# Stick-breaking attention: the running product over pairs of neighbouring keys, with GpSimd folding the odd key's factor into the even beta

## The chip, the cores and the metric

One NeuronCore of a Trainium2 chip runs the whole kernel in one launch. The metric is device time in microseconds (us), the median over runs of the same compiled kernel; lower is better.

## What is computed

A decoder block with two branches over 2048 positions and 1024 channels, all in float32. The branch that matters here is stick-breaking attention, with 8 heads of 128 channels. For each query t and each earlier key s,

```
logits    = einsum('bthd,bshd->bhts', q_blk, k) * head_dim ** -0.5
beta      = sigmoid(logits)
A[t, s]   = beta[t, s] * prod_{s < j < t} (1 - beta[t, j])
y_b       = A @ v
```

Keys at or after the query have weight 0. Before it come an RMSNorm, one input projection of 9 times 1024 columns and the other branch (gMLP); after it, the two output projections, a gated merge, a residual add and a final RMSNorm.

## The kernel before, in words

The kernel has four stages, one after the other: `norm_and_project` (the input projection, results stored to HBM as transposed arrays such as `k_T` and `vb_T`), `gate_and_project_a`, `attention`, and `merge_and_project_out`. TensorE multiplies float32 as three products of rounded parts (hi by hi, hi by lo, lo by hi), so most tiles exist as a pair hi and lo.

**Projection.** In `norm_and_project`, TensorE fills eight PSUM banks in turn; ScalarE takes each finished bank through a function into `o_sb` (L375 for the outputs that are stored alone, Copy for q, k and v) and issues its store.

**Attention.** For each head, the queries are cut into 16 rows of 128 (i = 0 to 15). Row i has (i + 1) * 128 keys, cut into pieces of up to 512 keys from the right (`z_pieces`). That makes 40 pieces per head, 320 in all: 28 of 512 keys and 4 each of 384, 256 and 128 keys per head. Each piece goes through five steps on four engines:

1. TensorE: the logits into one of three PSUM banks `z_ps` (L1287 to L1289), and on the diagonal block the mask (L1291).
2. ScalarE: sigmoid of the logits into `slot[i]` (L1177), which holds the betas; then sigmoid of the negated logits, which is 1 - beta, into `rest[i % 4]` (L1184). Each of the four `rest` buffers holds a whole row and ends in a column of ones. Before it writes the first piece of a row ScalarE waits until GpSimd has finished the row four earlier (`weighted`).
3. VectorE: `scan` (L1232), a running product from right to left in place over `rest`, which starts from the element to the right of the piece.
4. GpSimd: `weights` (L1143), beta times the product of everything to its right, in place in `slot[i]`.
5. TensorE: later, when all pieces of a row are done, it transposes 128x128 blocks of the row (L1320) into `t_ps`. ScalarE rounds them to `wT_hi` (L1207), VectorE takes the remainder `wT_lo` (L1244), and TensorE multiplies by v (L1331 to L1333). VectorE's gate product for a finished group of 512 queries is L1262.

VectorE also takes the lo part of the next head's q and k (L1221, eight pieces of 512 per head, both inputs in SBUF) and of v (L1240).

The order is written out by hand. `head_order` interleaves logits, splits and products of one head into one list, and every engine walks that same list: Z is a piece's logits and sigmoids, W its scan and weights, V and B the transposes, P the products, QK the splits, Y the gate product. Before the first head, 24 pieces (rows 0 to 11) run alone (`early`); within a head the last four rows run first and then the first twelve rows of the next head; the eighth head has only its own last 16 pieces. Each engine runs its instructions in order, so an instruction that waits holds up everything behind it. `P` is 128, `CW` and `ZW` are 512, `S` is 2048.

Of the kernel before, what the change touches and what calls it, by code (L numbers as in the profile page):

```python
# [17 lines left out]
ACT = mybir.ActivationFunctionType  # L18
# [128 lines left out]
def make_identity(pool, ident, zeroed, done):  # L147
# [4 lines left out]
                       pattern=[[-1, P]], channel_multiplier=1).then_inc(done, 1)  # L152

def norm_and_project(nc, x, norm_in, w_in, w_o_gmlp, s, carried):
# [13 lines left out]
    with ExitStack() as memory:  # L170
# [108 lines left out]
        def _(act):  # L279
# [83 lines left out]
            for n, (_, func, dst) in enumerate(single):  # L363
                before = UZ - 1 + n * PER

                def one_output(t):
                    for b in range(2):
                        for i in range(BANKS):
                            m, c = divmod(i, NC)
                            row = ((2 * t + b) * 2 + m) * P  # L370
                            step = 2 * (t + before) + b
                            act.wait_ge(pj.full[b][i], t + (before + 1))

                            wait_past(act, stored[i], 16 * (step - (0 if i < NC else 2 * (UZ - 1))))
                            act.activation(o_sb[:, i], banks[i][:, :], func).then_inc(pj.free[i], 1)  # L375
                            act.wait_ge(pj.free[i], step + 2)
                            act.dma_start(dst[bass.ds(row, P), c * CW:(c + 1) * CW], o_sb[:, i])\
                                .then_inc(stored[i], 16)

                if n == 0:  # L380
                    turns_from_first(act, PER, one_output)
                else:
                    with act.Fori(0, PER) as t:
                        one_output(t)
# [589 lines left out]
def attention(nc, w_o_sb, s, carried):  # L974
# [6 lines left out]
    W_BUFS = 4  # L981
    RESTS = 4
    assert PRODUCTS % W_BUFS == 0

    with ExitStack() as memory:
# [11 lines left out]

        rest = [sc.sb(f"rest{n}", [P, S + 1]) for n in range(RESTS)]

# [12 lines left out]
        z_full = sc.sem("z_full")  # L1012
        z_read = sc.sem("z_read")
        scanned = sc.sem("scanned")
        weighted = sc.sem("weighted")
# [114 lines left out]
        def _(pool):  # L1130
# [3 lines left out]

            pool.affine_select(out=mask[:, :], in_=mask[:, :], compare_op=ALU.is_gt, fill=MASKED, base=0,
                               pattern=[[-1, P]], channel_multiplier=1).then_inc(mask_done, 1)

            def weights(i, at, width, h, n):

                left = S - (i + 1) * P + at  # L1140
                a, r = slot[i][:, at:at + width], rest[i % RESTS]
                pool.wait_ge(scanned, PIECES * h + (n + 1))
                pool.tensor_tensor(a, a, r[:, left + 1:left + width + 1], ALU.mult).then_inc(weighted, 1)  # L1143

# [12 lines left out]
        def _(act):  # L1157
# [10 lines left out]
            def sigmoids(i, at, width, h, n):  # L1168

                src = z_ps[n % Z_BANKS][:, 0:width]  # L1170
                w = (i + 1) * P
                right = S - w + at
                act.wait_ge(z_full, PIECES * h + (n + 1))
                if at + width == w:
                    if not first_head(h):
                        act.wait_ge(turned, STEPS * h + (steps_until(i // QT) - STEPS))
                act.activation(slot[i][:, at:at + width], src, ACT.Sigmoid, scale=SCALE)  # L1177
                if at + width == w:

                    if i >= RESTS:  # L1180
                        act.wait_ge(weighted, PIECES * h + pieces_before(i - RESTS + 1))
                    elif not first_head(h):
                        act.wait_ge(weighted, PIECES * h + (pieces_before(NT + i - RESTS + 1) - PIECES))
                act.activation(rest[i % RESTS][:, right:right + width], src, ACT.Sigmoid, scale=-SCALE)\  # L1184
                    .then_inc(z_read, 1)

# [22 lines left out]
            for part in range(len(SPLITS)):  # L1209
                split_qk(0, part)  # L1210
            act.wait_ge(ones_set, RESTS)
            for n, e in enumerate(early):
# [4 lines left out]
        def _(dve):  # L1217
# [6 lines left out]
            def scan(i, at, width, h, n):  # L1224

                dve.wait_ge(z_read, PIECES * h + (n + 1))
                left = S - (i + 1) * P + at
                r = rest[i % RESTS]
                if at + width < (i + 1) * P:
                    dve.wait_ge(scanned, PIECES * h + n)  # L1230
                backwards = r[:, left:left + width][:, ::-1]
                dve.tensor_tensor_scan(out=backwards, data0=backwards, data1=backwards,  # L1232
                                       initial=r[:, left + width:left + width + 1], op0=ALU.mult,
                                       op1=ALU.bypass).then_inc(scanned, 1)
# [30 lines left out]
            for n in range(RESTS):  # L1265
                dve.memset(rest[n][:, S:S + 1], 1.0).then_inc(ones_set, 1)
            dve.wait_ge(ident_done, 1)
            dve.tensor_copy(ident_r[:, :], ident[:, :]).then_inc(consts, 1)
            dve.wait_ge(mask_done, 1)
            dve.tensor_copy(mask_r[:, :], mask[:, :]).then_inc(consts, 1)  # L1270
            for part in range(len(SPLITS)):
                split_qk(0, part)
# [375 lines left out]
```

## Time and profile before

| | |
|---|---|
| runs | 3024.46 us median of 3 (3023.23 to 3026.32) |
| profiled execution, first to last instruction | 3029.8 us |
| its own time around the span | not listed apart from the span |
| TensorE busy | 2814.0 us (93%) |
| VectorE busy | 1141.3 us (38%) |
| ScalarE busy | 881.2 us (29%) |
| GpSimd busy | 457.6 us (15%) |
| mean granted TensorE clock | 0.965 of full |

Busy time counts an instruction from its recorded start to its recorded end, time in which it is held up included. Two instructions that follow each other on VectorE or GpSimd without a wait can overlap by some hundredths of a microsecond in the records. "Idle before" is how long the engine stood empty before an instruction, with the instruction that released it behind the arrow. The shares above are over the whole span; attention fills only some 740 us of it.

### The profile page before, as it was taken

How to read it: one execution, taken by the hardware profiler on the slowest of the kernel's cores; microseconds unless marked ns; L12 is line 12 of the kernel's file. 1: busy time of each engine (PE TensorE's matmuls, PEld its weight loads, DVE VectorE, ACT ScalarE, POOL GpSimd, SP SyncE). 2: the span in 40 equal slices, each digit the busy share in tenths (PEclk: the TensorE clock that was granted, in tenths of full speed). 3: DMA queues.
4: the chain of work that ended last, by engine and by line, in shares of the span. 5: the costliest groups of instructions: out<-in, count | busy, mean ns of one | idle time of the engine just before them, and what ended most of it. 6: DMA issues, size and time to landing. Idle time of an engine off the chain costs nothing. (4 is left out here: it accounts for less than half of the span.)

```text
span 3029.8 us, 38475 instructions
## 1 busy us (share of the span) xinstructions
PE 2814.0 (93%) x14664; PEld 2392.2 (79%) x14664; DVE 1141.3 (38%) x1315; ACT 881.2 (29%) x1655; POOL 457.6 (15%) x432
## 2 busy tenths in 40 slices
PE   7999999999999999999996999688888888799998
PEld 5888888888888888888885999566666766689997
DVE  4310110000000000000003443999999999743333
ACT  5411111111111111111112221666766766521111
POOL 1111100000000000000001221644444444200000
PEclk9999999999999999999997999898989989999999
DMA  4310122122112212221115443111212110253332
GB/s 135 94 55 28 55 94 74 65 74 75 68 71 76 76 62 76 76 76 62 62 48 160 133 144 121 56 63 46 69 38 69 62 62 17 96 193 111 125 111 69
DMA packets 192585, 246.14 MB, mean 81 GB/s; under 512 B 9872, under 2 KB 141968, under 8 KB 189456
## 3 DMA queue, kind: packets, MB, share of 16 engines
q1 hardware_dynamic: 145040, 161.50, 16.7%
q10 hardware_dynamic: 47488, 83.90, 7.4%
q8 instruction: 32, 0.52, 0.1%
q14 instruction: 25, 0.20, 0.0%
HBM read 153.10 MB, written 92.27 MB: 81 GB/s over the span
## 5 line engine op out<-in xcount | busy, mean ns | idle before, releaser
L127 PE MATMUL in_bank<-in_h_hi,in_w_hi 128*128 128x512 f32 (+1 forms) x2304 | 897.7, 390 | 0.0
L129 PE MATMUL in_bank<-in_h_hi,in_w_lo 128*128 128x512 f32 (+1 forms) x2304 | 896.6, 389 | 0.0
L128 PE MATMUL in_bank<-in_h_lo,in_w_hi 128*128 128x512 f32 (+1 forms) x2304 | 896.5, 389 | 0.0
L118 DVE CAST in_w_hi<-in_w_stage 128x2048 fp32r<-128x2048 f32 x36 | 44.2, 1226 | 1292.6 <-PE in_bank L129 1292.6
L129 PEld LDWEIGHTS in_bank<-in_h_hi,in_w_lo 128*128 128x128 f32 x2304 | 432.6, 188 | 89.8
L127 PEld LDWEIGHTS in_bank<-in_h_hi,in_w_hi 128*128 128x128 f32 x2304 | 432.8, 188 | 89.5
L128 PEld LDWEIGHTS in_bank<-in_h_lo,in_w_hi 128*128 128x128 f32 x2304 | 432.6, 188 | 89.6
L1232 DVE TENSOR_TENSOR_SCAN att_rest<-att_rest 128x512 f32<-128x512 f32 (+3 forms) x320 | 445.5, 1398 | 36.1 <-ACT att_rest L1184 33.5
L375 ACT ACTIVATE in_o_sb<-in_bank 128x512 f32<-128x512 f32 x224 | 134.0, 598 | 1055.7 <-PE in_bank L129 1055.7
L1143 POOL TENSOR_TENSOR att_slot<-att_slot,att_rest 128x512 f32<-128x512 f32 (+3 forms) x320 | 343.0, 1077 | 378.7 <-DVE att_rest L1232 378.7
L1320 PE MATMUL att_t_ps<-att_ident,att_slot 128*128 128x128 f32 x1088 | 185.3, 288 | 61.6 <-DVE att_wT_lo L1244 51.6
L1177 ACT ACTIVATE att_slot<-att_z_ps 128x512 f32<-128x512 f32 (+3 forms) x320 | 173.1, 541 | 189.4 <-PE att_z_ps L1291 128.9
L1320 PEld LDWEIGHTS att_t_ps<-att_ident,att_slot 128*128 128x128 f32 x1088 | 128.1, 145 | 117.2 <-DVE att_wT_lo L1244 85.9
L1244 DVE TENSOR_TENSOR att_wT_lo<-att_t_ps,att_wT_hi 128x512 fp32r<-128x512 f32 (+1 forms) x320 | 185.7, 586 | 7.3 <-ACT att_wT_hi L1207 7.2
L610 POOL MEMSET a_minus_half<- 128x1 f32 x1 | 0.1, 98 | 1220.6 <-POOLq L47 1220.6
L1207 ACT ACTIVATE att_wT_hi<-att_t_ps 128x512 fp32r<-128x512 f32 (+1 forms) x320 | 172.5, 543 | 38.4 <-PE att_t_ps L1320 37.0
L1184 ACT ACTIVATE att_rest<-att_z_ps 128x512 f32<-128x512 f32 (+3 forms) x320 | 172.2, 539 | 2.4 <-POOL att_slot L1143 2.3
L1287 PE MATMUL att_z_ps<-att_k_hi,att_q_hi 128*128 128x512 f32 (+3 forms) x320 | 128.6, 402 | 45.0 <-DVE att_k_lo L1221 44.1
L1331 PE MATMUL att_y_ps<-att_wT_hi,att_v_hi 128*128 128x512 f32 (+1 forms) x320 | 147.6, 461 | 17.5 <-DVE att_wT_lo L1244 17.5
L1563 PE MATMUL b_p_ps<-b_y_hi,b_wo_hi 128*128 128x256 f32 x512 | 145.8, 285 | 14.5 <-DVE b_y_lo L1504 14.5
L838 PE MATMUL a_p_ps<-a_ya_hi,a_wo_hi 128*128 128x256 f32 x512 | 147.3, 288 | 4.0 <-DVE a_ya_lo L724 4.0
L839 PE MATMUL a_p_ps<-a_ya_lo,a_wo_hi 128*128 128x256 f32 x512 | 145.7, 285 | 0.0
(116 smaller groups left out, 3698.4 us busy)
## 6 DMA issues: line engine op xcount, KB each, us to landing
in_w_stage<-in_w_in SPq DMA_DIRECT2D x72, 512.0 KB, 4.4
carried_buffer<-in_x SPq DMA_DIRECT2D x32, 512.0 KB, 3.5
uz_T<-in_o_sb ACTq DMA_DIRECT2D x32, 256.0 KB, 2.7
va_T<-in_o_sb ACTq DMA_DIRECT2D x32, 256.0 KB, 2.4
q_T<-in_o_sb ACTq DMA_DIRECT2D x32, 256.0 KB, 2.4
k_T<-in_o_sb ACTq DMA_DIRECT2D x32, 256.0 KB, 2.4
vb_T<-in_o_sb ACTq DMA_DIRECT2D x32, 256.0 KB, 2.4
zb_T<-in_o_sb ACTq DMA_DIRECT2D x32, 256.0 KB, 2.4
```

Of the source, the lines that this page charges most:

```text
L127: pe.matmul(bank[:, :], hi, self.act_hi[:, k, cols], start=(k == 0), stop=False)
L128: pe.matmul(bank[:, :], hi, self.act_lo[:, k, cols], start=False, stop=False)
L129: mm = pe.matmul(bank[:, :], lo, self.act_hi[:, k, cols], start=False, stop=(k == KT - 1))
L838: pe.matmul(out, wo_hi[:, j, ks], ya_hi[:, b, j], start=(j == 0), stop=False)
L1143: pool.tensor_tensor(a, a, r[:, left + 1:left + width + 1], ALU.mult).then_inc(weighted, 1)
L1177: act.activation(slot[i][:, at:at + width], src, ACT.Sigmoid, scale=SCALE)
L1184: act.activation(rest[i % RESTS][:, right:right + width], src, ACT.Sigmoid, scale=-SCALE)\
L1207: act.activation(wT_hi[k % W_BUFS][:, c0:], t_bank(t)[:, c0:], ACT.Copy).then_inc(hi_copied, 1)
L1232: dve.tensor_tensor_scan(out=backwards, data0=backwards, data1=backwards, initial=r[:, left + width:left + width + 1], op0=ALU.mult, op1=A ...
L1244: dve.tensor_tensor(wT_lo[n][:, c0:], t_bank(t)[:, c0:], wT_hi[n][:, c0:].bitcast(F32), ALU.subtract).then_inc(lo_copied, 1)
L1320: ins = pe.transpose(out, slot[i][:, kt * P:(kt + 1) * P], ident[:, :])
L1331: pe.matmul(bank[:, c0:], v_hi[:, ks], hi[:, c0:], start=(kt == 0), stop=False)
```

## The change

The keys are stored apart by parity: inside each block of 128 keys the 64 even ones come first, then the 64 odd ones. ScalarE writes `k_T` and `vb_T` in that order when it empties the PSUM banks, and the mask is built in that order. `rest` becomes six buffers of one piece each instead of four of one row each. VectorE first multiplies the even and the odd half of a piece of `rest` into `pairs` (half as many columns, four buffers of a row each, ending in a column of ones), waits for that on its own semaphore, and then scans `pairs`. The wait for GpSimd's work on the row four earlier moves from ScalarE to VectorE; ScalarE now waits until the piece six earlier has been read by VectorE (`paired`) and GpSimd (`folded`). GpSimd first multiplies the even betas by the odd neighbour's 1 - beta (the fold, which needs only ScalarE's output), and after the scan multiplies all betas of the piece by the product of the pairs to their right, each of which is read twice through a stride of 0.

```diff
+def by_parity(keys):
+    return keys.rearrange("p (b m t) -> p b t m", t=2, m=P // 2)
...
+def by_parity_to(keys):
+    return keys.rearrange("p (b t m) -> p b t m", t=2, m=P // 2)
...
 def norm_and_project(nc, x, norm_in, w_in, w_o_gmlp, s, carried):
...
-                            act.activation(o_sb[:, i], banks[i][:, :], func).then_inc(pj.free[i], 1)
+                            if dst in (s["k_T"], s["vb_T"]):
+                                act.activation(by_parity_to(o_sb[:, i]), by_parity(banks[i][:, :]), func)\
+                                    .then_inc(pj.free[i], 1)
+                            else:
+                                act.activation(o_sb[:, i], banks[i][:, :], func).then_inc(pj.free[i], 1)
...
-        rest = [sc.sb(f"rest{n}", [P, S + 1]) for n in range(RESTS)]
+        rest = [sc.sb(f"rest{n}", [P, ZW]) for n in range(R_BUFS)]
+        pairs = [sc.sb(f"pairs{n}", [P, S // 2 + 1]) for n in range(RESTS)]
...
             def weights(i, at, width, h, n):
-                left = S - (i + 1) * P + at
-                a, r = slot[i][:, at:at + width], rest[i % RESTS]
+                left = (S - (i + 1) * P + at) // 2
+                nb, half = width // P, width // 2
+                a = slot[i][:, at:at + width].rearrange("p (b t m) -> p b t m", t=2, m=P // 2)
+                r = rest[n % R_BUFS][:, 0:width].rearrange("p (b t m) -> p b t m", t=2, m=P // 2)
+                pool.wait_ge(z_read, PIECES * h + (n + 1))
+                pool.tensor_tensor(a[:, :, 0], a[:, :, 0], r[:, :, 1], ALU.mult).then_inc(folded, 1)
                 pool.wait_ge(scanned, PIECES * h + (n + 1))
-                pool.tensor_tensor(a, a, r[:, left + 1:left + width + 1], ALU.mult).then_inc(weighted, 1)
+                pool.wait_ge(folded, PIECES * h + (n + 1))
+                after = pairs[i % RESTS][:, left + 1:left + half + 1].rearrange("p (b m) -> p b m", m=P // 2)
+                pool.tensor_tensor(a, a, after.unsqueeze(2).to_broadcast([P, nb, 2, P // 2]), ALU.mult)\
+                    .then_inc(weighted, 1)
...
                 act.activation(slot[i][:, at:at + width], src, ACT.Sigmoid, scale=SCALE)
-                if at + width == w:
-                    if i >= RESTS:
-                        act.wait_ge(weighted, PIECES * h + pieces_before(i - RESTS + 1))
-                    elif not first_head(h):
-                        act.wait_ge(weighted, PIECES * h + (pieces_before(NT + i - RESTS + 1) - PIECES))
-                act.activation(rest[i % RESTS][:, right:right + width], src, ACT.Sigmoid, scale=-SCALE)\
-                    .then_inc(z_read, 1)
+                before = last_user(n, PIECES, R_BUFS)
+                if before >= 0 or not first_head(h):
+                    act.wait_ge(folded, PIECES * h + (before + 1))
+                    act.wait_ge(paired, PIECES * h + (before + 1))
+                act.activation(rest[n % R_BUFS][:, 0:width], src, ACT.Sigmoid, scale=-SCALE).then_inc(z_read, 1)
...
             def scan(i, at, width, h, n):
                 dve.wait_ge(z_read, PIECES * h + (n + 1))
-                left = S - (i + 1) * P + at
-                r = rest[i % RESTS]
+                left, half = (S - (i + 1) * P + at) // 2, width // 2
+                q = pairs[i % RESTS]
+                r = rest[n % R_BUFS][:, 0:width].rearrange("p (b t m) -> p b t m", t=2, m=P // 2)
+                if at + width == (i + 1) * P:
+                    if i >= RESTS:
+                        dve.wait_ge(weighted, PIECES * h + pieces_before(i - RESTS + 1))
+                    elif not first_head(h):
+                        dve.wait_ge(weighted, PIECES * h + (pieces_before(NT + i - RESTS + 1) - PIECES))
+                dve.tensor_tensor(q[:, left:left + half].rearrange("p (b m) -> p b m", m=P // 2),
+                                  r[:, :, 0], r[:, :, 1], ALU.mult).then_inc(paired, 1)
+                dve.wait_ge(paired, PIECES * h + (n + 1))
                 if at + width < (i + 1) * P:
                     dve.wait_ge(scanned, PIECES * h + n)
-                backwards = r[:, left:left + width][:, ::-1]
+                backwards = q[:, left:left + half][:, ::-1]
                 dve.tensor_tensor_scan(out=backwards, data0=backwards, data1=backwards,
-                                       initial=r[:, left + width:left + width + 1], op0=ALU.mult,
+                                       initial=q[:, left + half:left + half + 1], op0=ALU.mult,
                                        op1=ALU.bypass).then_inc(scanned, 1)
```

## Rows read from the trace of the kernel before

**Rows 1.** Busy time by engine: the first pieces of attention, then its body.

```profile
core 0: us, PE busy (x) PEld busy (x) DVE busy (x) ACT busy (x) POOL busy (x), PEclk, DMA share, GB/s
...
1895.00:1940.00 45.00, 23.79 (x104) 17.62 (x104) 42.05 (x37) 26.88 (x62) 37.21 (x26) 0.77 0.13 53
1940.00:2640.00 700.00, 586.08 (x3161) 476.29 (x3161) 651.70 (x734) 465.67 (x993) 306.17 (x297) 0.92 0.17 57
```

**Rows 2.** Who waited for whom, 1940 to 2640 us: total us, times, longest.

```profile
POOL att_slot L1143 <- DVE att_rest L1232: 371.1, 272, 4.4
...
PEld att_t_ps L1320 <- DVE att_wT_lo L1244: 85.9, 98, 1.7
...
DVE att_rest L1232 <- ACT att_rest L1184: 32.2, 36, 1.3
```

**Rows 3.** VectorE in order of time in the body: start us, duration us, what.

```profile
2204.35 0.66 DVE L1244 TENSOR_TENSOR att_wT_lo<-att_t_ps,att_wT_hi 128x512 fp32r<-128x512 f32 x1
2204.93 1.75 DVE L1232 TENSOR_TENSOR_SCAN att_rest<-att_rest 128x512 f32<-128x512 f32 x1
2206.60 0.66 DVE L1244 TENSOR_TENSOR att_wT_lo<-att_t_ps,att_wT_hi 128x512 fp32r<-128x512 f32 x1
```

**Rows 4.** GpSimd in the same stretch.

```profile
2204.51 1.09 POOL L1143 TENSOR_TENSOR att_slot<-att_slot,att_rest 128x512 f32<-128x512 f32 x1 [1.16 <-DVE att_rest L1232]
```

**Rows 5.** VectorE instructions in order of time with no GpSimd work beside them.

```profile
1896.89 0.69 DVE L1221 TENSOR_TENSOR att_q_lo<-carried_buffer,att_q_hi 128x512 fp32r<-128x512 f32 x1
...
1941.02 1.27 DVE L1232 TENSOR_TENSOR_SCAN att_rest<-att_rest 128x512 f32<-128x512 f32 x1
...
1949.55 0.74 DVE L1232 TENSOR_TENSOR_SCAN att_rest<-att_rest 128x256 f32<-128x256 f32 x1
...
1984.80 1.02 DVE L1232 TENSOR_TENSOR_SCAN att_rest<-att_rest 128x384 f32<-128x384 f32 x1 [0.16 <-ACT att_rest L1184]
...
2212.55 0.48 DVE L1232 TENSOR_TENSOR_SCAN att_rest<-att_rest 128x128 f32<-128x128 f32 x1 [0.61 <-ACT att_rest L1184]
```

**Rows 6.** Order of time at a second place: VectorE, then GpSimd.

```profile
1999.93 2.01 DVE L1232 TENSOR_TENSOR_SCAN att_rest<-att_rest 128x512 f32<-128x512 f32 x1
...
1999.77 1.09 POOL L1143 TENSOR_TENSOR att_slot<-att_slot,att_rest 128x512 f32<-128x512 f32 x1 [1.50 <-DVE att_rest L1232]
```

**Rows 7.** Order of time among the first pieces: VectorE, then GpSimd.

```profile
1915.56 1.86 DVE L1232 TENSOR_TENSOR_SCAN att_rest<-att_rest 128x512 f32<-128x512 f32 x1
...
1914.33 2.01 POOL L1143 TENSOR_TENSOR att_slot<-att_slot,att_rest 128x512 f32<-128x512 f32 x1
...
1916.30 2.01 POOL L1143 TENSOR_TENSOR att_slot<-att_slot,att_rest 128x512 f32<-128x512 f32 x1
```

**Rows 8.** VectorE in the last stage; L1519 waits for L1517 on its own engine.

```profile
2803.27 0.42 DVE L1517 TENSOR_TENSOR b_gate<-b_p_ps,b_gate 128x256 f32<-128x256 f32 x1 [0.35 <-PE b_p_ps L1565]
2803.73 0.42 DVE L1519 TENSOR_TENSOR b_gate<-b_gate,carried_buffer 128x256 f32<-128x256 f32 x1
```

**Rows 9.** GpSimd in order of time: pieces of 256 and of 128 keys.

```profile
1993.62 0.64 POOL L1143 TENSOR_TENSOR att_slot<-att_slot,att_rest 128x256 f32<-128x256 f32 x1 [0.62 <-DVE att_rest L1232]
...
2213.12 0.41 POOL L1143 TENSOR_TENSOR att_slot<-att_slot,att_rest 128x128 f32<-128x128 f32 x1 [0.78 <-DVE att_rest L1232]
```

**Rows 10.** VectorE groups by form, all of attention: busy us, mean ns, idle.

```profile
L1232 DVE TENSOR_TENSOR_SCAN att_rest<-att_rest 128x512 f32<-128x512 f32 x224 | 358.8, 1603 | 8.1 <-ACT att_rest L1184 5.6
...
L1221 DVE TENSOR_TENSOR att_q_lo<-carried_buffer,att_q_hi 128x512 fp32r<-128x512 f32 x32 | 33.7, 1058 | 0.0
```

**Rows 11.** GpSimd L626, both operands as blocks of 128: ns min/median/max.

```profile
L626 POOL TENSOR_TENSOR a_y<-a_y,a_bias x16: 2357/2400/4323, 1638.6 to 1855.6; 128x1024 f32<-128x1024 f32 x16
```

**Rows 12.** GpSimd group by form in the projection stage, VectorE mostly idle.

```profile
L275 POOL TENSOR_TENSOR in_o_sb<-in_o_sb 128x512 f32<-128x512 f32 x24 | 33.7, 1405 | 227.5 <-ACT in_o_sb L356 227.5
```

**Rows 13.** ScalarE L375, 1000 to 1100 us, and its idle time, in us and times.

```profile
L375 ACT ACTIVATE in_o_sb<-in_bank x19: 598/598/601, 1000.8 to 1098.7; 128x512 f32<-128x512 f32 x19
...
  PE in_bank L129: 90.7, 19
```

More of the change, by code:

```diff
@@ L152, in make_identity, with in_parity @@
                        pattern=[[-1, P]], channel_multiplier=1).then_inc(done, 1)
+def by_parity(keys):
+    return keys.rearrange("p (b m t) -> p b t m", t=2, m=P // 2)
+def in_parity(keys):
+    return keys.rearrange("p (t m) -> p t m", t=2)
+def by_parity_to(keys):
+    return keys.rearrange("p (b t m) -> p b t m", t=2, m=P // 2)
 def norm_and_project(nc, x, norm_in, w_in, w_o_gmlp, s, carried):
@@ L982, in attention @@
     RESTS = 4
+    R_BUFS = 6
     assert PRODUCTS % W_BUFS == 0
@@ L1013, in attention @@
         z_read = sc.sem("z_read")
+        paired = sc.sem("paired")
+        folded = sc.sem("folded")
         scanned = sc.sem("scanned")
@@ L1133, in _ @@
             pool.wait_ge(mask_zeroed, 1)
-            pool.affine_select(out=mask[:, :], in_=mask[:, :], compare_op=ALU.is_gt, fill=MASKED, base=0,
-                               pattern=[[-1, P]], channel_multiplier=1).then_inc(mask_done, 1)
+            pool.affine_select(out=in_parity(mask[:, :]), in_=in_parity(mask[:, :]), compare_op=ALU.is_gt,
+                               fill=MASKED, base=0, pattern=[[-1, 2], [-2, P // 2]],
+                               channel_multiplier=1).then_inc(mask_done, 1)
             def weights(i, at, width, h, n):
-                left = S - (i + 1) * P + at
-                a, r = slot[i][:, at:at + width], rest[i % RESTS]
+                left = (S - (i + 1) * P + at) // 2
[4 more added lines that the diff above has]
+                pool.tensor_tensor(a[:, :, 0], a[:, :, 0], r[:, :, 1], ALU.mult).then_inc(folded, 1)
                 pool.wait_ge(scanned, PIECES * h + (n + 1))
-                pool.tensor_tensor(a, a, r[:, left + 1:left + width + 1], ALU.mult).then_inc(weighted, 1)
+                pool.wait_ge(folded, PIECES * h + (n + 1))
+                after = pairs[i % RESTS][:, left + 1:left + half + 1].rearrange("p (b m) -> p b m", m=P // 2)
+                pool.tensor_tensor(a, a, after.unsqueeze(2).to_broadcast([P, nb, 2, P // 2]), ALU.mult)\
+                    .then_inc(weighted, 1)
             def body(h, last):
@@ L1171, in sigmoids @@
                 w = (i + 1) * P
-                right = S - w + at
                 act.wait_ge(z_full, PIECES * h + (n + 1))
@@ L1210, in _ @@
                 split_qk(0, part)
-            act.wait_ge(ones_set, RESTS)
             for n, e in enumerate(early):
@@ L1265, in _ @@
             for n in range(RESTS):
-                dve.memset(rest[n][:, S:S + 1], 1.0).then_inc(ones_set, 1)
+                dve.memset(pairs[n][:, S // 2:S // 2 + 1], 1.0).then_inc(ones_set, 1)
             dve.wait_ge(ident_done, 1)
@@ L1270, in _ @@
             dve.tensor_copy(mask_r[:, :], mask[:, :]).then_inc(consts, 1)
+            dve.wait_ge(ones_set, RESTS)
             for part in range(len(SPLITS)):
```

## Prediction

> **What bounds the kernel now.** The change touches attention, so I read the busy time of that stage first. In its body, 1940 to 2640 us, VectorE is busy 651.7 of 700 us, TensorE 586.1, ScalarE 465.7, GpSimd 306.2 [rows 1]. The list of waits agrees: TensorE's weight loads for the transposes stand empty behind `wT_lo`, VectorE's last step before a product, for 85.9 us, while VectorE itself waits for its input for only 32.2 us. GpSimd waits 371.1 us for scans, so it has room [rows 2]. VectorE sets the pace, and what is spared or added in its queue moves the end. By busy time alone GpSimd looks like a free helper.
>
> The second question is what VectorE's busy time is made of. In order of time, a steady piece of 512 keys goes: `wT_lo` at 2204.35, scan at 2204.93 for 1.75 us, the next `wT_lo` at 2206.60, a period of 2.25 us [rows 3]. The same scan with no GpSimd work beside it takes 1.27 us [rows 5]. The other 0.48 us is a stall. GpSimd's multiply starts at 2204.51 [rows 4]; a scan that ends at 2206.68 and needs 1.27 us began its work at 2205.41, which is 0.90 us after the multiply's start. A second place says the same: multiply at 1999.77, scan issued at 1999.93 and 2.01 us long [rows 6], so it worked from 2000.67, again 0.90 us after the multiply's start. So the scan, which reads two operands from SBUF, and GpSimd's multiply exclude each other for most of the multiply. It goes the other way too: in the first pieces, scan behind scan, the multiply is recorded at 2.01 us and the scan at 1.86, and multiplies start 1.97 us apart [rows 7], which is 1.07 + 0.90. I take 1.07 us as the scan's share (1.27 less its fixed part, about 0.20) and 0.90 as the multiply's. `wT_lo` reads one operand from PSUM and stays at 0.66 us beside a multiply [rows 3, 4]. What this kernel has too little of is therefore not only VectorE's time but the turns that the two engines take, and the change adds GpSimd work there.
>
> **The change on VectorE.** The scan of 512 columns becomes one of 256: 0.74 us instead of 1.27 [rows 5]. Added is a multiply of 256 columns from SBUF. L1519, also two SBUF operands, takes 0.42 us at that width, and starts 0.04 us after the end of the instruction it waits for on its own engine [rows 8]. Alone, then: 0.42 + 0.04 + 0.74 = 1.20 against 1.27 us, a gain of 0.07 us per piece. Halving the scan brings almost nothing, since the pairing costs what the shorter scan spares.
>
> **The stalls.** Take the end of a scan as 0. The multiply of that piece starts at 0.08 (2204.51 against 2204.43 [rows 3, 4]) and excludes VectorE until 0.98. VectorE does `wT_lo`, then issues the pairing at 0.50, which stalls to 0.98 as the scan did before, works to about 1.25 and is recorded to 1.40. The scan could start at 1.44. But GpSimd is done with the multiply at 1.17 and has the next fold ready in its queue, since the fold needs only ScalarE's output. The fold has 256 columns. A GpSimd multiply goes from 0.41 us at 128 columns to 0.64 at 256 [rows 9] and 1.09 at 512 [rows 4], 1.77 ns a column, so 256 columns exclude for 0.45 us. It gets its turn when the pairing lets go, at 1.25, and holds to 1.70. The scan runs from 1.70 to 2.44. The period was 2.25, so the piece costs 0.19 us more: -0.07 for the shorter work and +0.26 for the fold's turn. The average piece stalls less than that one (mean scan 1603 ns, so 0.33 us [rows 10]), but that is the multiply's stall, which stays; the fold's comes on top. The other account agrees: where both engines are saturated, turns per piece go from 1.07 + 0.90 = 1.97 to 0.27 + 0.53 + 0.45 + 0.90 = 2.15 us, +0.18, and the 24 first pieces get that.
>
> **The sum.** 224 pieces of 512 at +0.19 are 43 us. Narrower ones go by the same lines (pairing 0.15 us + 1.05 ns a column, from 0.42 at 256 [rows 8] and 0.69 at 512 [rows 5]; scan 0.22 us + 2.06 ns; fold 1.77 ns, of which 0.19 us passes before the scan is ready). For 384 keys: 0.35 + 0.04 + 0.61 + 0.15 = 1.15 against 1.02. For 256: 0.28 + 0.04 + 0.48 + 0.04 = 0.84 against 0.74. For 128: 0.22 + 0.04 + 0.35 = 0.61 against 0.48. Together +0.36 for 32 of each, 12 us. The 56 splits that run beside GpSimd also read twice from SBUF: 1.06 us on average [rows 10] against 0.69 alone [rows 5], a stall of 0.37. GpSimd's turns rise from 0.90 of 2.25 us to 1.35 of 2.44, 1.38 times the share, so +0.14 each, 8 us. The sum is +63 us. On the profiled execution, span 3029.8 us, that is 3093; the median of the runs shown is 5.3 us shorter, so 3087.
>
> **What costs nothing.** ScalarE empties the projection's banks with a strided read for k and v: 64 instructions of 598 ns, and between 19 of them in 100 us it waited 90.7 us for TensorE [rows 13]. Even twice as long they stay under TensorE; without that cover, 64 times 0.6 is 38 us. No stores or loads are added or moved, so SP's queue is as before. ScalarE's removed wait on `weighted` was not felt, and its new waits reach back four to six pieces, some 9 us or more, behind work that GpSimd and VectorE do in order; behind them would stand the sigmoids and `wT_hi` copies. VectorE's new wait on `weighted` reaches back at least three pieces. If GpSimd lagged so far, `wT_lo` would be late behind it, and TensorE after it. TensorE's own instructions do not change.
>
> **What the trace does not show.** GpSimd has no instruction here that steps over blocks of 64 or reads through a stride of 0. Downwards, contiguous rows give 1.77 ns a column, and nothing suggests less. Upwards, L626 with blocks of 128 takes 2.40 us for 1024 columns at the median [rows 11], 2.2 ns a column beyond the 0.41 us of 128. A contiguous multiply of 512 in the projection takes 1.41 us [rows 12], longer than here by 0.32 with no VectorE work beside it, so GpSimd's fixed part isn't certain either. I take 1.77, since it is this very line in this stage. The scan of 256 and the pairing are bounded from below by the rows at that width.
>
> A rule bears on the turns. The Trainium skill, SBUF — State Buffer, section "Who interferes with whom", says that GpSimd and a VectorE instruction with two SBUF inputs contend, and that whoever starts first keeps the shared ports for its whole instruction. The trace agrees on who contends, and differs on how long: the scan worked 0.19 us before the multiply's recorded end. What the rule would give by whole records is the third rival.
>
> **Rivals.**
> - *The fold finds a free turn (faster), 0.13.* The price that decides is the 0.26 us; below 0.07 the change gains. The place is the gap under `wT_lo`, 0.58 us, where VectorE does not need a turn, but the multiply fills it, being released by the scan just ended. Where something else (a gate product, a v split) stands between, the fold can fit too. Were it always so: -0.07 for 224, and -0.02, +0.06 and +0.13 for 32 each, -10 us: 3014. A lesser share of free turns gives no change, 0.07.
> - *GpSimd is slower on blocks, 0.20.* At 2.2 ns a column the multiply excludes for 1.14 us and the fold for 0.57: pairing +0.24, scan +0.12, in all +0.55 per piece of 512, 123 us, half of the addition (0.18) on 96 narrower ones with the 12, 29 us, and the splits 10: 3187. Rows 11 speak for it, the flat L1143 against. The Trainium skill, GPSIMD Engine Reference, section 3.1, puts a two-input elementwise operation at about 2.6 cycles an element, which at its 1.2 GHz I estimate as 2.2 ns; L1143's 1.77 disagrees, L626 does not.
> - *Turns last for whole records, 0.03.* Pairing from 1.17 to 1.59, fold to 2.23, scan to 2.97: +0.72 us for 224, 161 us, with the rest about 3215. Against it: before, such a scan would have ended at 2206.87 and ended at 2206.68.
> - *The change doesn't shorten the scan.* If a scan cost the same at half the width it would add 0.5 us a piece; the widths in [rows 5] rule that out.
>
> **How the numbers follow.** The forecast, 3087, has a chance of 0.57. The faster case holds 0.13, no change 0.07, GpSimd slower on blocks 0.20 and whole records 0.03. Faster or slower by 0.2% (6 us) is about what a measurement of this kernel can tell. So faster 0.13, same 0.07, slower 0.80. The range takes in the no-gain case and reaches halfway and more into the slower GpSimd: 3012 to 3160.
>
> **What would show each step.** Scans of 256 near 0.74 us alone, with a mean of some 1.0; pairings of 0.42 alone, with a mean near 0.75; folds at 0.64 alone and longer beside VectorE; GpSimd busy over 600 us; the period of a steady piece 2.4 us and the idle time of transposes behind `wT_lo` longer. ScalarE in the projection may take longer and TensorE there must not wait. Wrong is the forecast if the pairing's or the scan's records show no stall, if folds exceed 0.7 us with VectorE idle, or if the body of attention is not some 60 us longer.

## The result, and the profile after

The changed kernel takes 3120.32 us (median of 4 runs, 3118.78 to 3122.11) against 3025.39 us for the kernel before in the same comparison. The ratio is 1.0311, with a 95% interval of 1.0295 to 1.0326: slower by 95 us. The forecast was 3087, slower by 63.

The page of the changed kernel: busy time, share of the span and instructions of each engine.

```profile
span 3120.4 us, 39891 instructions
...
PE 2836.5 (91%) x14664; PEld 2397.0 (77%) x14664; DVE 1233.5 (40%) x1635; ACT 885.6 (28%) x1655; POOL 683.2 (22%) x752
```

The profiled run took 3122.11 us around a span of 3120.4. VectorE's busy time rose by 92.2 us from 1141.3, GpSimd's by 225.6 from 457.6. By stretches (busy us of each engine, clock, DMA), which answer to [rows 1]:

```profile
core 0: us, PE busy (x) PEld busy (x) DVE busy (x) ACT busy (x) POOL busy (x), PEclk, DMA share, GB/s
...
1895.00:1940.00 45.00, 29.98 (x103) 21.51 (x103) 41.42 (x56) 28.46 (x63) 35.05 (x44) 0.68 0.15 56
1940.00:2640.00 700.00, 525.57 (x2755) 416.27 (x2756) 664.86 (x927) 418.66 (x895) 483.86 (x547) 0.92 0.15 49
```

In the same 700 us of attention, VectorE is a little fuller than before (664.9 us against 651.7) and TensorE is less busy (525.6 us against 586.1). Who waited for whom, 1940 to 2720 us (total, times, longest):

```profile
POOL att_slot L1175 <- DVE att_pairs L1269: 185.2, 272, 1.6
PEld att_t_ps L1358 <- DVE att_wT_lo L1281: 150.7, 149, 2.8
...
DVE att_pairs L1263 <- ACT att_rest L1214: 23.9, 29, 1.3
```

GpSimd's spare time behind scans shrank, and TensorE waits longer for `wT_lo`: 150.7 us over 780 us, against 85.9 over 700 in [rows 2]. A steady piece, VectorE in order of time (start, duration), which answers to [rows 3]:

```profile
2283.41 0.66 DVE L1281 TENSOR_TENSOR att_wT_lo<-att_t_ps,att_wT_hi 128x512 fp32r<-128x512 f32 x1
2283.99 0.95 DVE L1263 TENSOR_TENSOR att_pairs<-att_rest 128x256 f32<-128x256 f32 x1
2284.98 1.11 DVE L1269 TENSOR_TENSOR_SCAN att_pairs<-att_pairs 128x256 f32<-128x256 f32 x1
2286.01 0.66 DVE L1281 TENSOR_TENSOR att_wT_lo<-att_t_ps,att_wT_hi 128x512 fp32r<-128x512 f32 x1
```

and GpSimd, which answers to [rows 4]:

```profile
2283.57 1.10 POOL L1175 TENSOR_TENSOR att_slot<-att_slot,att_pairs 128x512 f32<-128x512 f32 x1 [0.62 <-DVE att_pairs L1269]
2284.62 0.92 POOL L1171 TENSOR_TENSOR att_slot<-att_slot,att_rest 128x256 f32<-128x256 f32 x1
2286.17 1.10 POOL L1175 TENSOR_TENSOR att_slot<-att_slot,att_pairs 128x512 f32<-128x512 f32 x1 [0.63 <-DVE att_pairs L1269]
```

The period from `wT_lo` to `wT_lo` is 2.60 us, where it was 2.25. The pairing is recorded at 0.95 us and needs 0.42; the scan at 1.11 and needs 0.75. The fold, issued 1.05 us after the multiply, is recorded at 0.92 us and needs 0.72 or 0.73 (both shown further below). Each of the three stands still for a while behind an instruction of the other engine. VectorE's groups in attention (count, busy us and mean ns, idle before) show the same on average; these answer to [rows 10], and the groups of 192 and 128 columns are left out:

```profile
L1269 DVE TENSOR_TENSOR_SCAN att_pairs<-att_pairs 128x256 f32<-128x256 f32 x224 | 237.1, 1058 | 7.9
L1263 DVE TENSOR_TENSOR att_pairs<-att_rest 128x256 f32<-128x256 f32 x224 | 184.5, 824 | 3.6 <-ACT att_rest L1214 3.5
...
L1249 DVE TENSOR_TENSOR att_q_lo<-carried_buffer,att_q_hi 128x512 fp32r<-128x512 f32 x32 | 33.8, 1061 | 0.0
...
L1249 DVE TENSOR_TENSOR att_k_lo<-carried_buffer,att_k_hi 128x512 fp32r<-128x512 f32 x32 | 26.7, 839 | 0.0
...
L1269 DVE TENSOR_TENSOR_SCAN att_pairs<-att_pairs 128x64 f32<-128x64 f32 x32 | 19.6, 613 | 1.1
...
L1263 DVE TENSOR_TENSOR att_pairs<-att_rest 128x64 f32<-128x64 f32 x32 | 13.9, 434 | 12.1 <-ACT att_rest L1214 11.9
```

VectorE's last gate product of attention moved from 2639.90 to

```profile
2730.30 0.69 DVE L1299 TENSOR_TENSOR att_y<-att_y_ps,att_zb 128x512 f32<-128x512 f32 x1 [1.47 <-PE att_y_ps L1371]
```

so by 90.4 us. The spans of the two profiled runs differ by 90.6 us, so the whole loss lies inside attention. ScalarE's strided copies in the projection are the same 598 ns as the plain ones (ns min/median/max, first and last start):

```profile
L391 ACT ACTIVATE in_o_sb<-in_bank x64: 598/598/601, 746.7 to 1089.3; 128x512 f32<-128x512 f32 x64
```

### The profile page after: what moved, and what is told of

Same layout as the page of the kernel before. It is cut to its first block and busy times, and to the rows that moved or that the text cites. A ratio compares the mean times of both kernels' runs of the same rounds, so it can differ in the third digit from the quotient of the medians.

```text
span 3120.4 us, 39891 instructions
## 1 busy us (share of the span) xinstructions
PE 2836.5 (91%) x14664; PEld 2397.0 (77%) x14664; DVE 1233.5 (40%) x1635; ACT 885.6 (28%) x1655; POOL 683.2 (22%) x752
## 5 line engine op out<-in xcount | busy, mean ns | idle before, releaser
L1175 POOL TENSOR_TENSOR att_slot<-att_slot,att_pairs 128x512 f32<-128x512 f32 (+3 forms) x320 | 317.5, 992 | 193.1 <-DVE att_pairs L1269 186.6
L1269 DVE TENSOR_TENSOR_SCAN att_pairs<-att_pairs 128x256 f32<-128x256 f32 (+3 forms) x320 | 305.0, 953 | 11.3
L394 ACT ACTIVATE in_o_sb<-in_bank 128x512 f32<-128x512 f32 x160 | 95.7, 598 | 745.9 <-PE in_bank L129 745.8
L1171 POOL TENSOR_TENSOR att_slot<-att_slot,att_rest 128x256 f32<-128x256 f32 (+3 forms) x320 | 263.4, 823 | 48.6 <-ACT att_rest L1214 48.5
L1358 PEld LDWEIGHTS att_t_ps<-att_ident,att_slot 128*128 128x128 f32 x1088 | 129.2, 147 | 185.2 <-DVE att_wT_lo L1281 150.7
L1263 DVE TENSOR_TENSOR att_pairs<-att_rest 128x256 f32<-128x256 f32 (+3 forms) x320 | 244.5, 764 | 24.7 <-ACT att_rest L1214 24.4
L1214 ACT ACTIVATE att_rest<-att_z_ps 128x512 f32<-128x512 f32 (+3 forms) x320 | 171.0, 535 | 12.1 <-POOL att_slot L1171 12.1
```

Of the source, the lines that this page charges most:

```text
L1171: pool.tensor_tensor(a[:, :, 0], a[:, :, 0], r[:, :, 1], ALU.mult).then_inc(folded, 1)
L1175: pool.tensor_tensor(a, a, after.unsqueeze(2).to_broadcast([P, nb, 2, P // 2]), ALU.mult)\
L1263: dve.tensor_tensor(q[:, left:left + half].rearrange("p (b m) -> p b m", m=P // 2), r[:, :, 0], r[:, :, 1], ALU.mult).then_inc(paired, 1)
L1358: ins = pe.transpose(out, slot[i][:, kt * P:(kt + 1) * P], ident[:, :])
```

## The experiments

Two theories were to be told apart. **Turns**: VectorE instructions with two SBUF operands and GpSimd instructions that read SBUF exclude each other, and the fold adds to that. The rivals: **the pairing** (an added instruction with a wait and strided operands costs by itself), and **GpSimd's time** (its queue holds the pace, whatever it does). Each kernel below was timed beside the kernel before on the same chip; the ratios are against that one. The kernel before took 3019.55 to 3025.39 us (medians) in these comparisons, so a difference between two kernels of different comparisons carries a few us of uncertainty.

**Without the fold.**

```diff
-                pool.wait_ge(z_read, PIECES * h + (n + 1))
-                pool.tensor_tensor(a[:, :, 0], a[:, :, 0], r[:, :, 1], ALU.mult).then_inc(folded, 1)
...
-                pool.wait_ge(folded, PIECES * h + (n + 1))
...
-                    act.wait_ge(folded, PIECES * h + (before + 1))
```

> The changed kernel with GpSimd's fold left out (the even betas lack their neighbour's factor), everything else kept. Theory (turns): the fold's turn at the shared reads is what stalls the scan; without it the scan of 256 is back at about 0.75 us, the pairing stays near 0.95 us, the steady period falls from 2.60 to about 2.25 us and the time to 3015 to 3040 us. Rival (the pairing itself, its wait and the strided operands cost): the time stays above 3090 us.

Measured: 3019.34 us, ratio 0.999 (0.9981 to 1.0). The pairing, its wait, the half scan, the strided copies and the new buffers cost nothing and gain nothing in sum. VectorE in order of time:

```profile
2202.06 0.67 DVE L1277 TENSOR_TENSOR att_wT_lo<-att_t_ps,att_wT_hi 128x512 fp32r<-128x512 f32 x1
2202.64 0.96 DVE L1259 TENSOR_TENSOR att_pairs<-att_rest 128x256 f32<-128x256 f32 x1
2203.63 0.75 DVE L1265 TENSOR_TENSOR_SCAN att_pairs<-att_pairs 128x256 f32<-128x256 f32 x1
2204.30 0.67 DVE L1277 TENSOR_TENSOR att_wT_lo<-att_t_ps,att_wT_hi 128x512 fp32r<-128x512 f32 x1
```

and GpSimd in the same stretch:

```profile
2202.22 1.09 POOL L1172 TENSOR_TENSOR att_slot<-att_slot,att_pairs 128x512 f32<-128x512 f32 x1 [1.15 <-DVE att_pairs L1265]
```

The scan is 0.75 us, unstalled, the pairing still 0.96 behind the multiply, the period 2.24 to 2.25. Without the fold the whole loss is gone. The groups show that the sum of nothing is made of a gain and a loss:

```profile
L1265 DVE TENSOR_TENSOR_SCAN att_pairs<-att_pairs 128x256 f32<-128x256 f32 x224 | 184.3, 823 | 7.9
L1259 DVE TENSOR_TENSOR att_pairs<-att_rest 128x256 f32<-128x256 f32 x224 | 153.9, 687 | 5.8 <-ACT att_rest L1210 4.9
```

With the gap of 40 ns a piece of 512 keys takes 1550 ns of VectorE where the scan took 1603, a gain of 12 us over 224 pieces. The 96 narrower pieces lose 22 us by the same sum over their groups (the narrowest takes 400 + 40 + 606 ns where its scan took 657). The splits are 6 us shorter, and the pairings wait 27.1 us for ScalarE where the scans waited 33.5.

**A GpSimd instruction of the same length that reads nothing**, in the fold's place.

```diff
-                pool.wait_ge(z_read, PIECES * h + (n + 1))
-                pool.tensor_tensor(a[:, :, 0], a[:, :, 0], r[:, :, 1], ALU.mult).then_inc(folded, 1)
+                pool.memset(filler[:, 0:width * 5 // 4], 0.0).then_inc(folded, 1)
```

> The changed kernel with the fold replaced by a GpSimd memset of a scratch tile, 1.25 times the piece's width, about 0.6 us for a full piece: GpSimd is occupied as long as by the fold, but reads nothing from SBUF (the fold's product is left out). Theory (turns are for reads): as without the fold, 3015 to 3050 us. Rival (GpSimd's time or its queue holds the pace, whatever it does): 3100 us and more, as the changed kernel.

Measured: 3021.85 us, ratio 0.9999 (0.9989 to 1.0008). GpSimd in order of time:

```profile
2203.74 1.09 POOL L1175 TENSOR_TENSOR att_slot<-att_slot,att_pairs 128x512 f32<-128x512 f32 x1 [0.57 <-DVE att_pairs L1269]
2204.77 0.63 POOL L1171 MEMSET att_filler<- 128x640 f32 x1
```

and VectorE:

```profile
2204.16 0.96 DVE L1263 TENSOR_TENSOR att_pairs<-att_rest 128x256 f32<-128x256 f32 x1
2205.15 0.75 DVE L1269 TENSOR_TENSOR_SCAN att_pairs<-att_pairs 128x256 f32<-128x256 f32 x1
```

The memset holds GpSimd for 0.63 us, nearly as long as an unstalled fold, just where the fold was, under the end of the pairing and the start of the scan, and the scan is 0.75 us. On average too, scans of 256 take 823 ns with the memset and 823 without it. GpSimd's time is not what costs here; its reading is. The Trainium skill, SBUF — State Buffer, section "Who interferes with whom", says that a VectorE instruction with two SBUF inputs contends with a GpSimd instruction that reads SBUF and not with one that only writes. This run agrees with it.

**The kernel before with one more GpSimd multiply**, of half the piece's width into a scratch tile.

```diff
+                pool.wait_ge(z_read, PIECES * h + (n + 1))
+                pool.tensor_tensor(filler[:, 0:width // 2], slot[i][:, at:at + width // 2], ident[:, 0:1].to_broadcast([P, width // 2]),
+                                   ALU.mult).then_inc(folded, 1)
                 pool.wait_ge(scanned, PIECES * h + (n + 1))
+                pool.wait_ge(folded, PIECES * h + (n + 1))
```

> The kernel before with one more GpSimd multiply of half a piece's width per piece, from slot into a scratch tile, placed and waited for as the fold is; VectorE's work untouched, output unchanged. Theory (turns): the extra multiply costs the kernel before about as much as the whole change did: each steady scan stalls some 0.3 us more, 3090 to 3130 us. Rival (the pairing costs, GpSimd has room: it idled 371 us): within 10 us of the kernel before, 3025 us.

Measured: 3093.49 us, ratio 1.0231 (1.0211 to 1.025). The size is as the theory had it, without any pairing, but the loss takes another form than I expected. The mean scan of 512 fell to 1473 ns; instead GpSimd was stalled, its groups (count, busy us, mean ns)

```profile
L1149 POOL TENSOR_TENSOR att_slot<-att_slot,att_rest 128x512 f32<-128x512 f32 x224 | 337.7, 1508 | 32.1
L1145 POOL TENSOR_TENSOR att_filler<-att_slot,att_ident 128x256 f32<-128x256 f32 x224 | 247.8, 1106 | 0.0
```

being 0.4 and nearly 0.5 us longer than alone, so that GpSimd fell behind (it is busy 584.0 of the 620 us from 1940 to 2560) and the wait before `rest` is overwritten was felt (waits, 1940 to 2600 us):

```profile
DVE att_rest L1238 <- ACT att_rest L1190: 100.0, 38, 5.4
ACT att_rest L1190 <- POOL att_slot L1149: 93.6, 25, 6.3
```

A scan of 512 keeps its turn for some 1.07 us (as worked out in the prediction), and GpSimd waits when it asks during it; in the changed kernel two shorter instructions stand in its place, and there VectorE loses more. The changed kernel's new buffers do spare it this wait. So this run shows what an added GpSimd read costs, not that it costs it in the same place. Nor can it by itself tell turns from GpSimd's time, since here GpSimd's queue did become the limit; the memset run does that.

**One SBUF operand less in the scan.** Its second operand is ignored (the second operator is a bypass). The next runs read it from PSUM. That takes a bank, so there is a control, the kernel before with two transpose banks instead of three (`T_BANKS = 2`):

> Control for the next two: the kernel before with two transpose banks in PSUM instead of three, which frees a bank. VectorE sets the pace, so the third bank should matter little: 3025 to 3060 us.

It took 3040.93 us, ratio 1.005 (1.0034 to 1.0066). With the operand moved:

```diff
-                dve.tensor_tensor_scan(out=backwards, data0=backwards, data1=backwards,
+                dve.tensor_tensor_scan(out=backwards, data0=backwards, data1=ones_ps[:, 0:width],
```

> The kernel before, two transpose banks, the scan's second operand (which the bypass ignores) read from the freed PSUM bank instead of from the same SBUF columns. Same arithmetic, same widths, one SBUF operand less. Theory (turns are between GpSimd's reads and VectorE instructions with two SBUF operands): the stall of 0.33 us per full scan vanishes, scans of 512 are 1.27 to 1.35 us beside a multiply, VectorE's period falls to about 1.8 us and TensorE becomes the bound: 2940 to 2980 us. Rival (any GpSimd work in SBUF stalls VectorE, or the stall is of writes): no change against the control.

Measured: 2955.91 us, ratio 0.9769 (0.9746 to 0.9793), 85 us below its control. VectorE in order of time:

```profile
2201.17 1.27 DVE L1233 TENSOR_TENSOR_SCAN att_rest<-att_rest,att_ones_ps 128x512 f32<-128x512 f32 x1
2202.36 0.66 DVE L1245 TENSOR_TENSOR att_wT_lo<-att_t_ps,att_wT_hi 128x512 fp32r<-128x512 f32 x1
2202.94 1.26 DVE L1233 TENSOR_TENSOR_SCAN att_rest<-att_rest,att_ones_ps 128x512 f32<-128x512 f32 x1
```

and GpSimd:

```profile
2202.52 1.09 POOL L1144 TENSOR_TENSOR att_slot<-att_slot,att_rest 128x512 f32<-128x512 f32 x1 [0.68 <-DVE att_rest L1233]
```

The multiply runs beside a scan as in [rows 3, 4], and the scan is 1.27 us instead of 1.75; the period is 1.77. Same arithmetic, same widths: the stall is a matter of where the second operand lies.

**The same edit in the changed kernel:**

> The changed kernel, two transpose banks, the scan's second operand from PSUM. Theory (turns): the fold no longer stalls the scan, only the pairing stalls on the multiply (about 0.5 us): steady period about 2.2 us, 3010 to 3040 us, so the change stays behind the kernel before with the same edit. Rival: no change against 3120 us.

Measured: 3014.78 us, ratio 0.996 (0.9949 to 0.9972), 105 us less than the changed kernel, and 59 us more than the kernel before with the same edit. The time is as I expected, the steady piece is not: it takes 1.94 us instead of 2.2, with the pairing recorded at 0.66 us, stalled by 0.24 and not by 0.5. The last run below shows much the same piece.

**Half a fold**, the fold over the first 32 of each 64 even keys, to find out when the pairing gives up its turn.

> The changed kernel with the fold over half of its columns (128 instead of 256 of a full piece; the other half of the even betas is left without its factor). It tells when the pairing gives up its turn. If at the end of its record (as the changed kernel's 2.60 us suggests), the fold starts at 1.41, holds 0.23 us and the steady scan stalls by 0.15 us: period 2.38 to 2.40 us, some 3045 to 3070 us. If after 0.27 us of columns, as the forecast had it, the fold is over before the scan could start: period 2.25 us, as without the fold, 3015 to 3025 us.

Measured: 3049.53 us (3042.05 to 3060.42), ratio 1.0075 (1.0053 to 1.0097). VectorE in order of time:

```profile
2292.97 0.66 DVE L1282 TENSOR_TENSOR att_wT_lo<-att_t_ps,att_wT_hi 128x512 fp32r<-128x512 f32 x1
2293.56 0.94 DVE L1264 TENSOR_TENSOR att_pairs<-att_rest 128x256 f32<-128x256 f32 x1
2294.53 0.83 DVE L1270 TENSOR_TENSOR_SCAN att_pairs<-att_pairs 128x256 f32<-128x256 f32 x1
```

and GpSimd:

```profile
2293.13 1.09 POOL L1176 TENSOR_TENSOR att_slot<-att_slot,att_pairs 128x512 f32<-128x512 f32 x1 [0.63 <-DVE att_pairs L1270]
2294.18 0.64 POOL L1171 TENSOR_TENSOR att_slot<-att_slot,att_rest 128x128 f32<-128x128 f32 x1
```

The same fold elsewhere, begun under a gate product, before VectorE asked for its turn:

```profile
2289.19 0.47 POOL L1171 TENSOR_TENSOR att_slot<-att_slot,att_rest 128x128 f32<-128x128 f32 x1
```

Alone the strided fold of 128 columns takes 0.46 or 0.47 us, not the 0.41 of a contiguous multiply [rows 9]. In the steady piece it is recorded at 0.64, so it began its work 0.18 us late, at 2294.36. The scan before, issued at 2292.22 for 0.83 us, ended at 2293.05, and that is again the 0: the pairing let go at 1.31. The scan is 0.83 us, stalled by 0.08, and the period is 2.32. So neither of my two figures was right: the pairing gives up its turn well before the end of its record (1.45), and the fold is longer than I had it. The time alone would have spoken for the first account, whose 3045 to 3070 us it meets; only the trace rules that account out. The four executions also spread over 18 us, and the trace is of the longest.

**Which bank to give up.** Two ways keep all three transpose banks in the kernel before: the second operand is the piece's own logits bank, which TensorE then may reuse only after the scan,

```diff
-                    pe.wait_ge(z_read, PIECES * h + (before + 1))
+                    pe.wait_ge(scanned, PIECES * h + (before + 1))
...
-                dve.tensor_tensor_scan(out=backwards, data0=backwards, data1=backwards,
+                dve.tensor_tensor_scan(out=backwards, data0=backwards, data1=z_ps[n % Z_BANKS][:, 0:width],
```

> The kernel before with all its banks; the scan's second, ignored operand is the piece's own logits bank, so TensorE may reuse that bank only after the scan instead of after ScalarE. No stall of scans, but logits wait up to 2 us longer for one of three banks: between 2935 us (banks suffice) and 3030 us (they hold the pace).

which took 2924.93 us, ratio 0.9671 (0.9655 to 0.9688); or a constant bank taken from the logits (`Z_BANKS = 2`, `T_BANKS = 3`):

> The kernel before, scan's second operand from a constant PSUM bank, the bank taken from the logits (two) instead of from the transposes (three). The control with two transpose banks lost 15 us, so if logits need their third bank less, 2940 to 2955 us; if more, above 2960 us.

2925.05 us, ratio 0.9672 (0.9656 to 0.9688). The piece's own logits bank again, with four logits banks and two transpose banks:

> As the last one, with four logits banks and two transpose banks. With a fourth bank the later release should be hidden: within 15 us of the variant with a constant bank, 2956 us.

2956.04 us, ratio 0.9775 (0.9759 to 0.9791). This met its expectation; the two before it came out faster than I had expected. The third transpose bank is worth 31 us here, a third logits bank nothing (2924.93 against 2925.05 with two), and a fourth nothing (2956.04 against 2955.91 with three, in the run with the constant bank and two transpose banks). The first of the three needs no other change and, level with the second, is the fastest kernel of this study: 100 us below the kernel before, 195 below the changed one. Its groups on VectorE:

```profile
L1232 DVE TENSOR_TENSOR_SCAN att_rest<-att_rest,att_z_ps 128x512 f32<-128x512 f32 x224 | 284.6, 1272 | 5.8 <-ACT att_rest L1184 3.7
...
L1221 DVE TENSOR_TENSOR att_q_lo<-carried_buffer,att_q_hi 128x512 fp32r<-128x512 f32 x32 | 33.8, 1061 | 0.0
```

The mean scan of 512 is 1272 ns with GpSimd beside it; the splits of q, still with two SBUF operands, keep their 1061 ns.

**The changed kernel with a constant bank taken from the logits** (two of those, three for the transposes):

> The changed kernel with the scan's second operand from a constant PSUM bank taken from the logits (two of those, three for the transposes), to be compared with the kernel before under the same edit, 2925 us. The pairing still has two SBUF operands and waits for the multiply's turn (steady period some 1.9 to 2.0 us against 1.77): 2970 to 3000 us, the change still behind by 45 to 75 us. If the turns of the scan were all that the change lost by, and the shorter scan a gain, it would come to 2925 us or below.

Measured: 3002.58 us, ratio 0.9942 (0.9925 to 0.9958), 78 us behind the kernel before under the same edit and just outside what I expected. GpSimd in order of time:

```profile
2281.24 1.10 POOL L1176 TENSOR_TENSOR att_slot<-att_slot,att_pairs 128x512 f32<-128x512 f32 x1
2282.30 0.72 POOL L1172 TENSOR_TENSOR att_slot<-att_slot,att_rest 128x256 f32<-128x256 f32 x1
2283.16 1.10 POOL L1176 TENSOR_TENSOR att_slot<-att_slot,att_pairs 128x512 f32<-128x512 f32 x1
```

and VectorE:

```profile
2282.08 0.67 DVE L1282 TENSOR_TENSOR att_wT_lo<-att_t_ps,att_wT_hi 128x512 fp32r<-128x512 f32 x1
2282.66 0.64 DVE L1264 TENSOR_TENSOR att_pairs<-att_rest 128x256 f32<-128x256 f32 x1
2283.34 0.75 DVE L1270 TENSOR_TENSOR_SCAN att_pairs<-att_pairs,att_ones_ps 128x256 f32<-128x256 f32 x1
```

GpSimd now goes from multiply to fold to multiply in 1.92 us with hardly a pause, and the pairing waits only 0.22 us. The fold begins here under `wT_lo`, ahead of the pairing, so its 0.72 us are its own. So where the scan no longer takes turns, GpSimd's own time is the next limit of the changed kernel's steady piece, at 1.92 us, where the kernel before needs 1.77 under the same edit. Over the whole body VectorE is still the fuller engine (588.9 of the 620 us from 1940 to 2560, GpSimd 496.2).

## Why the prediction was right, and where a size was off

**What bounds the kernel** held: VectorE's queue, of which a part is stalls against GpSimd. The run with one SBUF operand less shows it directly: 0.48 us of a steady scan was the stall.

**Gain from the shorter scan.** Forecast: -0.07 us a piece from 1.20 against 1.27 alone, if the multiply's stall stays. The steady piece gained nothing (2.24 or 2.25 without the fold against 2.25), because VectorE starts its pairing 1.03 us after the scan's end, not 0.98: the multiply keeps it out for 0.95 us instead of 0.90. That took most of the 0.07. On average a piece of 512 did gain 0.05 us, 12 us in all, but the narrower ones lost 22 us of VectorE's time by the pairing alone, where the forecast had them lose 5. In sum the time without the fold is that of the kernel before to 0.1%, where the forecast's own terms without the fold give 10 us less.

**The fold's turn** was the right mechanism, in the right place, and too small. The sequence of the forecast stands line by line: multiply at 0.08 after the scan's end, pairing issued at 0.50, fold at 1.13, scan issued at 1.49. The pairing let go at 1.32 (the fold's recorded end, 2285.54, less 0.73, from the scan's end at 2283.49, 0.08 ahead of the multiply), where I had 1.25: 0.05 of that is the multiply's. What failed is the term of the fold, 256 columns at 1.77 ns for 0.45 us: over strided blocks a fold takes 0.46 us at 128 and 0.72 or 0.73 at 256 columns, about 2.1 ns a column, and holds VectorE's scan to 1.85 instead of 1.70. The scan stalls by 0.36 us where I had 0.26. Of the 0.16 us by which the period was 2.60 and not 2.44, 0.08 is the fold's own length, 0.05 the multiply's, 0.02 the pairing's and 0.01 the scan's (0.75 for 0.74). Over the kernel the fold cost some 100 us, the changed kernel against the one without it, where the forecast's terms for it (224 times 0.26, 6 for the narrow pieces, 8 for the splits) make 72.

**The sum.** Pieces of 512: by the means, pairing 824 + gap 40 + scan 1058 - 1603 = +319 ns, times 224 = 71 us, where the forecast had 43. For the narrowest, 434 + 40 + 613 - 657 = +430 ns, where it had +0.13 us; all 96 narrower pieces together cost some 44 us instead of 12, and half of that is there without the fold. I costed them with multiplies and folds of their own width; in the list they stand between wide pieces, and an instruction of 64 columns waits for a neighbour's multiply of 512. A pairing of that kind in the half-fold run is recorded at 0.88 us, against 0.23 for one in the last run (GpSimd, then VectorE); scans of 64 columns take 613 ns on average, against 0.35 us for one alone:

```profile
2295.45 1.09 POOL L1176 TENSOR_TENSOR att_slot<-att_slot,att_pairs 128x512 f32<-128x512 f32 x1 [0.63 <-DVE att_pairs L1270]
...
2295.74 0.88 DVE L1264 TENSOR_TENSOR att_pairs<-att_rest 128x64 f32<-128x64 f32 x1
```

The splits were to cost 8 us and gave back 5 (mean 950 ns over both kinds, against 1033; the 1.06 us of the forecast was the mean of q's alone). Those three are 110 us. VectorE waited 9 us less for ScalarE than before (24.4 us against 33.5, by the pages); the other 11 us between this sum and the 90 us of attention were not traced to a step. So the total is nearer to the forecast than its terms are: the two kinds of piece cost 60 us more than forecast, and some 33 us of that were offset by splits, waits and the part that was not traced. That is luck, not precision.

**A sign of being wrong came.** The prediction said that it would be wrong if folds exceeded 0.7 us with VectorE idle. The nearest case in the changed kernel is a fold that starts while VectorE is in a `wT_lo` and so has its turn at once:

```profile
2212.62 0.73 POOL L1171 TENSOR_TENSOR att_slot<-att_slot,att_rest 128x256 f32<-128x256 f32 x1
```

The loss in attention, 90 us and not some 60, is the second such sign. The others did not come: pairing and scan show their stalls.

**What cost nothing** held: the strided copies at 598 ns, no longer waits in the projection, and ScalarE's new waits, 12.1 us on the page and not in the way.

**The rivals.** A free turn for the fold did not come about in the steady piece. GpSimd slower on blocks was right for the fold (2.1 ns a column against the rival's 2.2) and wrong for the multiply: through a stride of 0 it is 1.09 us for 512 columns, as before. I had priced the two as one, at +0.55 us a piece; the steady piece came at +0.35, between the forecast's 0.19 and this. Turns for whole records, 3215, was wrong: VectorE starts 0.15 us before the multiply's recorded end, the fold 0.13 us before the pairing's, and the scan 0.20 us before the fold's. The whole-instruction lock of the Trainium skill, SBUF — State Buffer, section "Who interferes with whom", fits only if the last 0.13 to 0.20 us of a record are not counted to it.

## What to carry to other kernels

Before work is moved to an engine that looks idle, look at what that engine reads while the busy one works: a VectorE instruction recorded longer beside GpSimd than alone is a stall that the added work will lengthen. Count the SBUF operands of VectorE's instructions; where one of two can lie in PSUM, or is ignored as in this scan, moving it may be worth more than shortening the instruction. And price a step by the neighbours that it will have in the queue, not by instructions of its own size.

## What was not expected of the hardware

The operand that a bypass ignores still counts: moving it alone took the mean scan of 512 from 1603 to 1272 ns. On GpSimd a multiply that steps over blocks of 64 costs about 2.1 ns a column (0.46 us at 128, 0.73 at 256), one whose second operand is read twice through a stride of 0 no more than a contiguous one (1.09 us for 512). A GpSimd memset of 640 columns ran beside two-operand instructions of VectorE without stalling them: the mean scan is 823 ns with it and without it. Why the same multiply of 512 columns takes GpSimd 1.41 us in the projection [rows 12] and 1.09 us here stays open.
